# Who makes the high half of a weight: from GpSimd to ScalarE, in a two-layer hybrid block on one Trainium2 core

## The reference

```
h = rms_norm(h_res, pre_mix_g); proj = h @ w_in            # q1 q2 k1 k2 v u
o = rms_norm(diff_attention(q1, q2, k1, k2, v, lam), subln_g) * (1 - lam_init)
y = s5_ssm(u, ...); y = gelu(y); y = rms_norm(y * sigmoid(y @ w_glu + b_glu), ssm_out_g)
h_res = h_res + rms_norm(concat(o, y) @ w_out, post_mix_g)
f = (silu(h @ w_gate) * (h @ w_up)) @ w_down               # h = rms_norm(h_res, pre_ffn_g)
h_res = h_res + rms_norm(f, post_ffn_g)
proj = rms_norm(x, norm_mix_w) @ w_in_2                    # second layer, x = h_res[16:]
x = x + concat(ret_out, rwkv7_mix(proj[2048:], ...)) @ w_o
x = x + (silu(hf @ w_gate) * (hf @ w_up)) @ w_down         # hf = rms_norm(x, norm_ffn_w)
x = x + (p @ w_ple_up) * sigmoid(rms_norm(x, norm_ple_w) @ w_ple_gate)
return rms_norm(x, final_norm_w)
```

## Time and profile before

| | |
|---|---|
| three timed executions | 3446.54, 3443.70 and 3434.99 us, median 3443.7 |
| the profiled execution | span 3446.0 us from the first to the last instruction; its time with what lies around the span is not given apart, and the slowest of the timed three is 0.5 us above the span |
| busy: PE, PEld, DVE, ACT, POOL | 3106.2, 2393.9, 1673.5, 854.1, 1991.6 us |
| granted TensorE clock, mean | 0.944 |
| phases, read from the units' first uses | first part to 546 us, phase 1 to 1200, phase 2 to 2060, phase 3 to 2960, last stretch to 3446 |

### The profile page before, as it was taken

The page is one execution under the profiler, slowest core; times in us unless marked ns, Lnnn a source line. Parts: engine busy times, 40 slices in busy tenths (PEclk is TensorE's granted clock), DMA queues, the critical chain, the costliest instruction groups (busy, mean ns, idle before and its releaser), DMA issues.

```text
span 3446.0 us, 47777 instructions
## 1 busy us (share of the span) xinstructions
PE 3106.2 (90%) x19536; PEld 2393.9 (69%) x19536; DVE 1673.5 (49%) x2264; ACT 854.1 (25%) x1591; POOL 1991.6 (58%) x1076
## 2 busy tenths in 40 slices
PE   6987878799998879989999989998999988999997
PEld 4765646577776657767777767776777766788875
DVE  5844543444442551666656553646565564222333
ACT  3111123322221341123332223122323332100012
POOL 5820322554654656746665747755666765677872
PEclk9888889899999989999999999998999999999998
DMA  4343323222222434322221244332222222332231
GB/s 154 114 130 97 102 71 110 89 68 80 74 68 80 141 133 151 104 74 74 84 81 59 84 153 140 118 95 74 84 71 85 79 71 68 128 98 92 92 104 55
DMA packets 158027, 329.99 MB, mean 96 GB/s; under 512 B 34960, under 2 KB 74064, under 8 KB 157808
## 3 DMA queue, kind: packets, MB, share of 16 engines
q1 hardware_dynamic: 58752, 213.94, 19.2%
q10 hardware_dynamic: 99056, 112.99, 10.2%
HBM read 281.89 MB, written 44.97 MB: 95 GB/s over the span
## 4 chain that ended last, share of the span: by engine, by line
PE 76%; DVE 15%; ACT 3%; ACTq 2%; issue 2%; DMA 1%; POOL 0%; DVEq 0%
PE ps L1814 31%; PE ps L1855 12%; PE ps L1843 12%; PE ps L1665 2%; DVE acc_dense L2250 2%; PE ps L1576 2%; PE ps L1546 1%; DVE act_lo L2250 1%; DVE xn_dense L2257 1%; DVE ffh_lo L2930 1%; PE ps L2049 1%; DVE added L2250 1%; ACTq L965 1%; PE ps L1586 1%; PE ps L1693 1%
## 5 line engine op out<-in xcount | busy, mean ns | idle before, releaser
L559 POOL TENSOR_TENSOR w_hi<-w_raw,ones 128x1024 fp32r<-128x1024 f32 x408 | 805.6, 1975 | 1175.9 <-DMA w_raw<-weights 1172.7
L561 POOL TENSOR_TENSOR w_lo<-w_raw,w_hi 128x1024 fp32r<-128x1024 f32 x408 | 1019.3, 2498 | 32.0
L1814 PE MATMUL ps<-act_hi,w_hi 128*128 128x512 f32 x1696 | 703.9, 415 | 13.6 <-ACT qk_raw L674 8.1
L1814 PE MATMUL ps<-act_lo,w_hi 128*128 128x512 f32 x1696 | 678.4, 400 | 0.0
L1814 PE MATMUL ps<-act_hi,w_lo 128*128 128x512 f32 x1696 | 674.5, 398 | 0.0
L1814 PEld LDWEIGHTS ps<-act_hi,w_hi 128*128 128x128 f32 x1696 | 324.1, 191 | 108.5 <-issue 16.6
L1814 PEld LDWEIGHTS ps<-act_hi,w_lo 128*128 128x128 f32 x1696 | 323.7, 191 | 75.0
L1814 PEld LDWEIGHTS ps<-act_lo,w_hi 128*128 128x128 f32 x1696 | 324.1, 191 | 67.0 <-issue 1.7
L2250 DVE TENSOR_TENSOR acc_dense<-acc_dense,ps 128x512 f32<-128x512 f32 x352 | 242.0, 688 | 227.9 <-PE ps L1843 179.0
L1843 PE MATMUL ps<-w_hi,ffh_hi 128*128 128x512 f32 x704 | 296.1, 421 | 55.9 <-DVE acc_dense L2250 54.4
L1843 PE MATMUL ps<-w_hi,ffh_lo 128*128 128x512 f32 x704 | 282.4, 401 | 0.0
(11 more groups left out here) (371 smaller groups left out, 4389.1 us busy)
## 6 DMA issues: line engine op xcount, KB each, us to landing
w_raw<-weights SPq DMA_DIRECT2D x408, 512.0 KB, 3.5
rw<-rw_t ACTq DMA_DIRECT2D x24, 256.0 KB, 2.4
rw<-lora_t ACTq DMA_DIRECT2D x24, 256.0 KB, 2.0
row<-x ACTq DMA_DIRECT2D x8, 512.0 KB, 3.9
row_dense<-x ACTq DMA_DIRECT2D x8, 512.0 KB, 5.5
row_mix<-res ACTq DMA_DIRECT2D x8, 512.0 KB, 7.5
res<-row_mix ACTq DMA_DIRECT2D x8, 512.0 KB, 5.0
acc_dense<-res ACTq DMA_DIRECT2D x8, 512.0 KB, 5.6
```

The lines of the kernel that those rows point to most:

```text
L559: pool.tensor_tensor(w_hi[:, s], raw, ones[:, 0:1].to_broadcast([P, 1024]), MUL).then_inc(w_hi_made, 1)
L561: pool.tensor_tensor(w_lo[:, s], raw, w_hi[:, s].bitcast(F32), SUB).then_inc(w_ready, 1)
L1814: mm = pe.matmul(out, ws[w][:, s, P * k:P * k + P], acts[a][:, k, x], start=(k, w, a) == (0, 0, 0), stop=(k, w, a) == (KT - 1, 1, 0))
```

## The change

ACT takes over line 559 for the last 378 of the 408 units (`W_START` is 30, the start of phase 1), as an activation with the function Copy, 128x1024, from `w_raw` to `w_hi`. POOL keeps both operations for the first 30 units and makes only `w_lo` for the others, when ACT has counted up `w_hi_made`. The place of a rounding among ACT's other work is written out by the program: after each event, ACT rounds the units up to three past those started, but no further than the slots allow that were free four events ago (`W_AHEAD`, `W_BEHIND`, and the new lists of ends). POOL splits at the same events, now in phase 1 too, and after its own work of the event. The last stretch has a list of its own (`EVENTS[4]`).

```diff
+    def ff_ends(f):
+        return [[ff_unit(f, "down", 2 * m), ff_unit(f, "down", 2 * m + 1)] if kind == "down" and part == 2 * HALF - 1 else
+                [ff_unit(f, kind, m)] if kind != "down" and part == 3 else [] for kind, m, part in FF_CHUNKS]
...
-    EVENTS, PHASE_START = {}, {}
...
+    W_START, W_AHEAD, W_BEHIND = len(ORDER), 3, 4
+    EVENTS, ended, made_ready = {}, [W_START] * W_BEHIND, [W_START + W_AHEAD]
+
+    def event(side, h, starts, ends):
+
+        ORDER.extend((h, u) for u in starts)
+        assert len(ORDER) <= made_ready[-1]
+        ended.append(ended[-1] + len(ends))
+        made_ready.append(min(len(ORDER) + W_AHEAD, ended[-W_BEHIND] + SLOTS))
+        return side, made_ready[-1]
...
@@ -556,7 +580,8 @@
                 pool.wait_ge(w_landed[s], 16 * (pos // SLOTS + 1))
-                pool.tensor_tensor(w_hi[:, s], raw, ones[:, 0:1].to_broadcast([P, 1024]), MUL).then_inc(w_hi_made, 1)
+                if pos < W_START:
+                    pool.tensor_tensor(w_hi[:, s], raw, ones[:, 0:1].to_broadcast([P, 1024]), MUL).then_inc(w_hi_made, 1)
                 pool.wait_ge(w_hi_made, pos + 1)
                 pool.tensor_tensor(w_lo[:, s], raw, w_hi[:, s].bitcast(F32), SUB).then_inc(w_ready, 1)
@@ -642,14 +667,12 @@
-        split_to(20)
-        split_to(PHASE_START[2] + 4)
-        for phase, h in ((2, 0), (3, 1)):
-            mix = mixing(h)
-            for side, started in EVENTS[phase]:
-                split_to(started + 4)
+        split_to(W_START + W_AHEAD)
+        for phase, mix in ((1, pieces(len(heads_starts))), (2, mixing(0)), (3, mixing(1))):
+            for side, ready in EVENTS[phase]:
                 if side == "mix":
                     next(mix)
+                split_to(ready)
         split_to(len(ORDER))
@@ -1439,6 +1462,16 @@
+        rounded = [W_START]
+
+        def round_to(n):
+
+            for pos in range(rounded[0], min(n, len(ORDER))):
+                s = pos % SLOTS
+                act.wait_ge(w_landed[s], 16 * (pos // SLOTS + 1))
+                fn(w_hi[:, s], w_raw[:, s], ACT.Copy).then_inc(w_hi_made, 1)
+                rounded[0] = pos + 1
@@ -1469,13 +1502,21 @@
+        act.wait_ge(w_ready, W_START)
+        round_to(W_START + W_AHEAD)
         for phase, mix, dense in ((1, heads_half(1), first_dense(0)), (2, mixing(0), first_dense(1)), (3, mixing(1), dense_half(0))):
-            for side, _ in EVENTS[phase]:
+            for side, ready in EVENTS[phase]:
                 next(mix if side == "mix" else dense)
+                round_to(ready)
...
-        for _ in dense_half(1):
+        last = dense_half(1)
+        for _, ready in EVENTS[4]:
+            next(last)
+            round_to(ready)
+        round_to(len(ORDER))
+        for _ in last:
             pass
```

More of the change, by code:

```diff
@@ L464, in out_starts, with token_ends, out_ends @@
         return [[us[4 * j + uu]] if k == 0 else [] for j, uu, k in OUT_ORDER]
+    def ff_ends(f):
+        return [[ff_unit(f, "down", 2 * m), ff_unit(f, "down", 2 * m + 1)] if kind == "down" and part == 2 * HALF - 1 else
+                [ff_unit(f, kind, m)] if kind != "down" and part == 3 else [] for kind, m, part in FF_CHUNKS]
+    def token_ends(us):
+        return [[u] if i == HALF - 1 else [] for u in us for i in range(HALF)]
+    def out_ends(us):
+        return [[us[4 * j + uu]] if k == HALF - 1 else [] for j, uu, k in OUT_ORDER]
     def norm_within(starts):
@@ L489, in build @@
                     + token_starts(range(U_PLE, U_PLE + 10)) + [[]] * NORM_STEPS)
+    first_ends = norm_within(out_ends(range(U_OUT, U_OUT + 8))) + ff_ends(0)
+    dense_ends = (norm_within(out_ends(range(U_WO, U_WO + 8))) + ff_ends(1) + [[]] * NORM_STEPS
+                  + token_ends(range(U_PLE, U_PLE + 10)) + [[]] * NORM_STEPS)
     def spread(total, n):
@@ L521, in build @@
     ORDER = [(0, u) for u in range(U_V, U_GLU)] + [(0, u) for u in range(U_V)] + [(1, u) for u in range(U_V, U_GLU)] + [(0, U_GLU), (0, U_GLU + 1)]
-    EVENTS, PHASE_START = {}, {}
-    for phase, h, mix, dense in ((1, 1, heads_starts, first_starts), (2, 0, mix_starts, first_starts), (3, 1, mix_starts, dense_starts)):
-        EVENTS[phase], PHASE_START[phase], done = [], len(ORDER), 0
-        for step, n in zip(mix, FILLS[phase]):
[L526 to L530, removed]
+    W_START, W_AHEAD, W_BEHIND = len(ORDER), 3, 4
[6 more added lines that the diff above has]
+        return side, made_ready[-1]
+    for phase, h, mix, dense, ends in ((1, 1, heads_starts, first_starts, first_ends), (2, 0, mix_starts, first_starts, first_ends),
+                                       (3, 1, mix_starts, dense_starts, dense_ends)):
+        EVENTS[phase], done = [], 0
+        for step, n in zip(mix, FILLS[phase]):
+            EVENTS[phase].append(event("mix", h, step, step))
+            for i in range(done, done + n):
+                EVENTS[phase].append(event("dense", 1 - h, dense[i], ends[i]))
             done += n
         assert done == len(dense) and len(mix) == len(FILLS[phase])
-    ORDER += [(1, u) for chunk in dense_starts for u in chunk]
+    EVENTS[4] = [event("dense", 1, *chunk) for chunk in zip(dense_starts, dense_ends)]
+    assert ended[-1] == len(ORDER)
     AT = {key: pos for pos, key in enumerate(ORDER)}
```

## The result

The changed kernel takes 3394.85 us in the median of four executions (3383.7 to 3409.39), the kernel before 3441.92 (four executions, 3434.99 to 3446.54). The ratio is 0.9868 [0.9841, 0.9894]: 1.3% or 45 us (36 to 55) faster, where I had forecast 0.7% or 24 us. The direction was right, the size was half of what came.

The account below looks back on a forecast made before the run. PE was taken as the bound, busy 3106 of 3446 us, so only shorter PE stalls could help: 3446 - 28 - 5 + 5 + 4 = 3422 us, 3420 against the median; the forecast's own range was 3400 to 3433.

Parts of the forecast that it names:

- Removed: the multiplications, 28 us: DVE instructions with two SBUF operands no longer wait for POOL's 378 multiplications: 28 us gained, 0 to 37 possible.
- the discount: Only three quarters of 37 us counted, since some DVE instructions spared the multiplication will meet a subtraction: 28 us.
- more comes back: Rival: PE's vanishing stalls also give back clock, 23 us on top, with the full 40 for 28: 3390 us, chance 0.20.
- my four times: The forecast 3420 us (chance 0.50) and rivals: more 3390 (0.20), nothing 3440 (0.18), slower 3480 (0.12).
- Moved: the subtraction, 5 us gained: Feed-forward: POOL's subtraction now follows ACT's rounding, so a prompt `ffh_lo` ends before it: 5 us gained, at worst 8 lost.
- Added: the roundings, 5 us lost: 378 roundings on ACT delay what is queued behind them; little falls on the chain: 5 us lost, upper bound 110.
- slower: Rival: ACT becomes the late engine and 60% of 110 us of uncovered lateness reach PE: 3480 us, chance 0.12.
- The start of phase 1, 4 us: PE waits for the first rounding and subtraction, partly instead of for the keys: 3.9 us lost, up to 5 more.
- Not in the sum: the new order of POOL: POOL's RWKV-7 work would begin at most 4 us later, with 4 to 110 us until its use: charged nothing.
- what should be seen: `ffh_lo` near 800 ns, DVE down 120 us or more, PE idle about 210, ACT near 1255, start stall some 10 us.

Follow-up runs that it names:

- Kernel 4: The changed kernel, but POOL keeps both parts for the first six units of phase 1 and ACT begins with the seventh: 3391.89 us, ratio 0.9861.
- experiment 5: The changed kernel with POOL's subtraction made in two instructions of 128x512 for all 408 units: 3358.19 us, ratio 0.9753.
- runs 1: The changed kernel, but POOL multiplies the same high part again between ACT's rounding and its own subtraction: 3473.41 us, ratio 1.0102.
- run 2: The changed kernel's events, but POOL makes both parts for all units and ACT rounds no weight: 3460.96 us, ratio 1.0053.
- runs 5 and 8: The changed kernel with POOL's subtraction cut into two instructions of 128x512 (5: 3358.19 us) or four of 128x256 (8: 3348.01 us, ratio 0.9721).

## Why the prediction was right in direction and wrong in size

The excess, and what of it lies on the chain that ended last, over six kernels. "On the chain" sums each DVE instruction's excess where the chain, followed from step to step, runs through it. Kernel 4 reads like the changed one; in the others the chain, followed from the end, breaks off at 1577 us or later and gives no such sum.

| kernel | ratio | excess at `w_hi`, `w_lo` | of it on the chain | PE idle | half clock |
|---|---|---|---|---|---|
| before | 1 | 116, 181 | 49 + 86 = 135 | 240 | 253 |
| order alone (2) | 1.0053 | 113, 199 | 47 + 94 = 142 | 249 | 264 |
| before in halves (6) | 0.9851 | 76, 108 | 24 + 49 = 73 | 199 | 215 |
| changed | 0.9868 | 0, 151 | 0 + 70 = 70 | 194 | 217 |
| ACT from phase 2 (7) | 0.9825 | 11, 141 | 9 + 64 = 73 | 197 | 207 |
| changed, halves (5) | 0.9753 | 0, 89 | 0 + 27 = 27 | 163 | 180 |

(us; the last two columns from phase 1 on, behind the stall at its start.)

*Removed: the multiplications, 28 us. This is the step that failed; the runs show 70 to 81 us in its place.* The first half of it held: 120 us of excess by squares of the lengths, 116 measured. What failed is how much of that counts. I spread the collisions evenly over DVE's work, 8.7% of the 425 us of its chain time, 37 us, and then took three quarters, because "some DVE instructions spared the multiplication will meet a subtraction". In the table 49 of the 116 us lie on the chain, 42%, where by my estimate 31% of DVE's busy time do (425 of 1375 us): DVE collides more where PE waits for it than elsewhere. And the discount had the wrong sign. With the multiplication gone the excess at subtractions did not rise but fell, from 181 to 151 us, and on the chain from 94 to 70 (order alone to changed). From before to its halves the chain's excess fell by 62 us and the time by 51, from the changed kernel to its halves by 43 and 40, and from order alone to changed by 72 and 64, with ACT's work of 17 us added in the second, so 81 without it. What is taken off the chain comes back by 0.8 to 1.1 of its length in these three steps. Part of that is clock. Behind the stall at its start the rest of the run takes 2841 us in the trace of the changed kernel and 2900 in that of before: 46 of the 59 us are PE's idle time, and 13 are PE's busy time, which grew shorter because half clock ruled for 36 us less. (The profiled execution lost 20 us ahead of that, 12 in the stall and 8 in the unchanged first part.) That is the rival "more comes back", whose 3390 us is the nearest of my four times; I gave it 0.20 because no row told which gaps would vanish. Its nearness is in part luck: it had 40 + 5 + 23 = 68 us of gain, clock included, and 9 us of costs, where the steps below have 81 and 35. None of the experiments separates clock from idle time either.

*Moved: the subtraction, 5 us gained.* Its excess on the chain fell by 86 - 70 = 16 us (30 in all), but not for the reason that I gave. `ffh_lo`, on which I had rested it, collides more with subtractions than before: 28 us of its excess begin beside or run into one, where it was 20; the pair in experiment 5 is such a case. The sum fell only with the multiplication gone: with the order alone it is 94. The pair in the earlier trace rows suggests why: of two POOL instructions back to back DVE waits for the first, has one turn, and waits for the second. That was not tried by itself.

*Added: the roundings, 5 us lost.* 17 us by runs 1 and 2, with late weights in it, and 19 for as much again. My count took only lateness on the chain as it was; that the chain moves to what is late is the likely reason, and was not followed up. The 66 us of the rival "slower" did not come.

*The start of phase 1, 4 us.* The stall was as forecast (11.73 us); its removal is worth 2 us by the time and 6.6 by the traces, not to be told from 4.

*Not in the sum: the new order of POOL, 18 us lost.* I had charged it nothing, since POOL's RWKV-7 work had 4 to 110 us until its use. POOL splits behind that work now, but late weights are not what costs (0.67 us in run 2). By the table the chain's excess is 7 us and PE's idle time 9 us above the kernel before, and half clock rules 11 us longer; why, stays open.

Taken as steps between measured kernels: 3443 + 18 (order) + 17 (ACT's roundings) - 81 (multiplications) = 3397. Each step is the difference of two of the same four ratios, so that they add up to the changed kernel says nothing for them. Forecast were 0, 5 + 4 and -28 - 5. The forecast's gain was 48 us too small and its costs 26 us too small; that it missed the total by only 22 is luck.

Of what should be seen, DVE's busy time (down by 167 us, at least 120), ACT's (1225, 1255), and the start stall came as written; PE's idle time fell further than written, to 194 us and not 210. `ffh_lo` did not come: 1029 ns, not 800. I had written that above 1000 would mean that the subtraction does the harm alone. It does not: in the kernel before, the 40 us of `ffh_lo` divide evenly between the two operations, 20 and 20, and for the whole kernel the multiplication was worth 70 to 81 us, while the subtraction kept another 40 and then 11 us, which runs 5 and 8 took out.

## What to carry to other kernels

When GpSimd works beside VectorE, compare each VectorE form's mean with its shortest, sum the excess *on the chain*, and count it in full (0.8 to 1.1 of it came back here). The cheapest cure is to cut GpSimd's instructions before moving them: halves in the kernel before brought what the whole change brought, and halves and quarters on top of the change 1.15% and 1.5%. Both together brought most (3.1%), since the cut alone ran into GpSimd's own time at quarters (1.7%). Stop cutting while GpSimd's time for one unit is still well below the pace at which TensorE uses the units (3.3 us of 5.6 was good, 4.4 was worse, 5.9 was the bound), and leave the work where it was in stretches with few collisions.

## What the runs showed of the hardware

- A GpSimd subtraction of 128 partitions takes 2460, 1341, 772 and 486 ns for 1024, 512, 256 and 128 columns: from each size to the next, two halves cost some 0.2 us more than the whole, so by this estimate an instruction has about 0.2 us of its own, and 78 ns pass between two that wait for each other.
- The longest VectorE instruction of 128x512 with two SBUF operands followed these lengths in the changed kernel and its three cuts (2931, 1823, 1195 and 999 ns, 691 undisturbed), while the adds with a PSUM operand had 688 ns in the mean in every kernel.
